# The first 128 tokens' experts start beside the last seven query tiles, in a ring of six buffers

## The chip, the core and the metric

The kernel runs on one core of one Trainium2 chip. The time is that of the device in microseconds, for one execution; 3375.86 us is the median of three (3374.03 to 3380.77). TensorE is called PE in the profile, VectorE DVE, ScalarE ACT, GpSimd POOL, and SP issues most plain loads. A GpSimd queue starts the gathers.

## What is computed

A transformer block with attention, then a second block of gated recurrences, and at its end a layer of product-key experts for 512 tokens of 1024 numbers. Only the last part matters here, cut from the reference:

```python
def _peer(x, w_pq, sub_keys, expert_u, expert_v):
    xf = x.reshape(n_tok, d)
    q = (xf @ w_pq).reshape(n_tok, P_HEADS, 2, P_DHALF)
    s = jnp.einsum('thpd,phkd->thpk', q, sub_keys)
    top_s, top_i = lax.top_k(s, P_TOPK)
    cand_s = (top_s[:, :, 0, :, None] + top_s[:, :, 1, None, :]).reshape(n_tok, P_HEADS, P_TOPK * P_TOPK)
    cand_i = (top_i[:, :, 0, :, None] * N_KEYS + top_i[:, :, 1, None, :]).reshape(...)
    best_s, pos = lax.top_k(cand_s, P_TOPK)
    idx = jnp.take_along_axis(cand_i, pos, axis=-1)
    gate = jax.nn.softmax(best_s)
    ...
    u = expert_u[it]
    h = jax.nn.gelu(jnp.einsum('td,tkd->tk', xt, u), approximate=False)
    v = expert_v[it]
    return jnp.einsum('tk,tkd->td', gt * h, v)
```

and around it `x = x + _peer(_rmsnorm(x, norm2), ...)`, then `_rmsnorm(x, final_norm)`. There are 8 heads, 128 keys in each half, 16 best pairs per head, so 128 experts for each token, out of 16384, each with a row u and a row v of 1024 float32.

## The kernel before

Tokens are taken 128 at a time, one to a partition: four token tiles (`TT`), each with 128 gathers (`PAIRS`). Gather number e brings for each of the 128 tokens the u and v row of its e-th expert, 8 KB per partition. A token tile has four parts (`PARTS`) of 32 gathers, one part for two heads, so there are 16 parts (`NPARTS`).

*Queries.* `project` makes 16 query tiles of 24 matmuls each (line 399 to 401). Weights come in chunks of 512 KB, one to a tile, into a ring of four (`ring`, SP); ScalarE rounds a chunk to its upper half (`upper`, line 956), GpSimd subtracts for the lower (`lower`, line 1962), and that must be there before TensorE's tile. ScalarE's `tile()` waits for a tile to be done and then makes the upper half two chunks further on; then it copies the queries from PSUM to `qpk`. `key_scores(n)` (line 886) makes the scores of part n, from query tiles 0 to 3 for part 0, 4 to 7 for part 1, and so on; the next token tile uses them again in the same order. `first_scores` calls it for parts 0 and 1 behind tiles 4 and 8.

*Top-k on VectorE.* `best_keys(n)` (from line 1859) finds the best keys of a part, `best_pairs(n)` (from line 1878) the best sums, the gates and the expert indices; in it VectorE waits for ScalarE's exponential (`gate_exp`, line 1386), which stands behind query tiles 9 and 13 for parts 0 and 1. Parts 0 and 1 run beside the query tiles.

*Between.* A meeting of PE, ACT and DVE (`meet(…, 19)`). ScalarE before it loads `wide`, an identity with zeros about it, then `final_norm` into `fin_g`, and waits for each. Then `by_tokens` transposes the normalised tokens of all four token tiles (line 907) and `tok_copy` copies them (line 1403) to `h2tok`, which lies in the weight ring.

*Experts.* Eight buffers, `uv[:, 0..7]`, each 2048 float32 per partition. For gather number e: GpSimd waits until the products of gather e - 8 are done (`v_used`) and issues (line 2000). VectorE takes them in pairs: two dot products of u rows with the tokens (line 1938), ScalarE's Gelu of both (line 1412), then two diagonal matrices with gelu times gate (line 1943); TensorE multiplies each with the v rows, two halves of 512 columns (line 930, four instructions of the trace for each gather), and sums in PSUM. The first four gathers may start once part 0 has its indices; the fifth waits for all transposes (`tok_mm`). They stand in GpSimd's program behind `lower_all`, all lower halves. `best_keys(n + 2)` runs after the first half of part n's pairs, `best_pairs(n + 2)` after the second. The residual goes into the same sum, by six matmuls with `wide` of 512 columns at the start of a token tile (line 924) and two at its end (line 935); ScalarE and VectorE then normalise and scale (`scale_out`) while the next token tile runs.

Where buffers lie: `uv[:, 0..3]` in two slots of the arena that are free by then; `uv[:, 4..7]` over the normalised tokens and their lower parts, which query tiles and transposes still read.

## Time and profile before

| | us |
|---|---|
| median of three runs | 3375.86 |
| the profiled execution | 3369.78 |
| its span | 3368.0 |
| PE busy | 2824.0 (84%) |
| DVE busy | 1806.6 (54%) |
| ACT busy | 918.1 (27%) |
| POOL busy | 1068.8 (32%) |
| line 1938, dot products, x512 | 618.9 |
| line 930, products with v, x2048 | 979.5 |
| line 2000, gathers, x512: GpSimd's time | 556.5 |

The query tiles begin near 1905 us of the span and the expert loop near 2020; it lasts to 3353. An engine's busy time says what it did; what it waited for stands in the idle time before an instruction, in brackets with the releaser. GpSimd's time for a gather is that of its issue; the rows land later. Numbers of pairs count from 0: pair p is gathers 2p and 2p + 1, and pair 63 is the last of the first token tile.

### The profile page before, as it was taken

The page shows a single profiled execution, that of the slowest core. Times are in us where ns is not written, and L with a number is a line of the kernel's source. Part 1 is how long each engine was busy: PE and PEld are TensorE (multiplying, and loading weights), DVE is VectorE, ACT ScalarE, POOL GpSimd, SP SyncE. Part 2 cuts the span into 40 slices and gives each one's busy share as a digit, 9 for nine tenths or more (in the row PEclk, how much of TensorE's full clock was granted, in tenths as well). Part 3 has the DMA queues.
Part 4 walks back from the last instruction along what each step waited for, and adds up shares of the span by engine and source line. Part 5 has one row for each costly group of instructions (what it writes and reads, how often), then busy time and mean ns, then how long its engine had stood idle before and what let it go on. Part 6 is the DMA issues. An engine that isn't in the chain of part 4 may idle for free.

```text
span 3368.0 us, 32768 instructions
## 1 busy us (share of the span) xinstructions
PE 2824.0 (84%) x11178; PEld 1867.2 (55%) x11178; DVE 1806.6 (54%) x3673; ACT 918.1 (27%) x1517; POOL 1068.8 (32%) x722
## 2 busy tenths in 40 slices
PE   5988899998998988999789987777777777777776
PEld 3866588785667976779767663333333333333332
DVE  1056233303666633239633237777777777777765
ACT  3244422223655134233543321111111111111100
POOL 2300244441000002345233334444444444444342
PEclk9999999998998999999999989998998899999999
DMA  3200122222110001221112229999999999999998
GB/s 118 78 20 1 51 94 93 87 100 106 69 63 13 1 26 63 88 94 45 63 69 86 90 106 413 396 396 395 408 396 396 401 412 396 398 398 407 401 400 341
DMA packets 115300, 671.68 MB, mean 199 GB/s; under 512 B 16232, under 2 KB 17512, under 8 KB 49008
## 3 DMA queue, kind: packets, MB, share of 16 engines
q0 software_dynamic: 73728, 536.90, 38.9%
q1 hardware_dynamic: 31536, 114.83, 9.6%
q10 hardware_dynamic: 9920, 18.42, 1.6%
q8 instruction: 70, 1.15, 0.1%
q14 instruction: 46, 0.38, 0.0%
HBM read 663.78 MB, written 6.32 MB: 199 GB/s over the span
## 4 chain that ended last, share of the span: by engine, by line
PE 44%; issue 24%; DMA 14%; DVE 13%; ACT 3%; POOL 2%; DVEq 0%; ACTq 0%; PEldq 0%; POOLq 0%; PEld 0%
PE ps L930 14%; DMA arena<-in_experts,arena 13%; PE ps L399 8%; PE ps L400 8%; PE ps L401 8%; POOL ring_r L1962 2%; DVE arena L1938 1%; PE ps L565 1%; DVE arena L1790 1%; PE ps L537 1%; PE ps L456 1%; DVE arena L1943 1%; DVE arena L1789 1%; DVE arena L1772 1%; PE ps L563 1%
## 5 line engine op out<-in xcount | busy, mean ns | idle before, releaser
L930 PE MATMUL ps<-arena 128*128 128x512 f32 x2048 | 979.5, 632 | 319.6 <-DVE arena L1943 319.5
L1962 POOL TENSOR_TENSOR ring_r<-ring,w_hi 128x1024 fp32r<-128x1024 f32 x191 | 470.2, 2462 | 1422.9 <-ACT w_hi L956 1299.0
L930 PEld LDWEIGHTS ps<-arena 128*128 128x128 f32 x2048 | 399.9, 202 | 892.6 <-DVE arena L1943 447.5
L2000 POOL DMA_INDIRECT arena<-in_experts,arena x512 | 556.5, 1087 | 793.5 <-PE ps L930 737.6
L1938 DVE SCALAR_TENSOR_TENSOR arena<-arena,ring 128x1024 f32<-128x1024 f32 x512 | 618.9, 1224 | 265.9 <-DMA arena<-in_experts,arena 237.6
L399 PE MATMUL ps<-n_hi,w_hi 128*128 128x512 f32 (+1 forms) x1264 | 503.5, 398 | 50.6 <-DVE low L1441 20.5
L401 PE MATMUL ps<-n_hi,ring_r 128*128 128x512 f32 (+1 forms) x1264 | 493.6, 391 | 0.0
L956 ACT ACTIVATE w_hi<-ring 128x1024 fp32r<-128x1024 f32 x175 | 185.1, 1058 | 651.2 <-PE ps L401 642.2
L400 PE MATMUL ps<-slot_r,w_hi 128*128 128x512 f32 x896 | 359.1, 401 | 0.0
L1412 ACT ACTIVATE hgel<-hdot 128x2 f32<-128x2 f32 x256 | 52.0, 203 | 1109.2 <-DVE arena L1938 1109.2
L399 PEld LDWEIGHTS ps<-n_hi,w_hi 128*128 128x128 f32 x1264 | 240.6, 190 | 132.1 <-issue 50.8
L401 PEld LDWEIGHTS ps<-n_hi,ring_r 128*128 128x128 f32 x1264 | 240.8, 191 | 54.2
L1943 DVE TENSOR_SCALAR arena<-con,hgel,arena 128x128 f32<-128x128 f32 x512 | 157.5, 389 | 107.9 <-ACT hgel L1412 107.7
L400 PEld LDWEIGHTS ps<-slot_r,w_hi 128*128 128x128 f32 x896 | 173.2, 193 | 39.0 <-issue 1.4
L400 PE MATMUL ps<-low,w_hi 128*128 128x512 f32 (+1 forms) x496 | 188.1, 379 | 0.0
L1461 DVE SCALAR_TENSOR_TENSOR arena<-arena,par 128x512 f32<-128x512 f32 x16 | 11.8, 746 | 185.2 <-ACT arena L996 185.2
L400 PEld LDWEIGHTS ps<-low,w_hi 128*128 128x128 f32 x496 | 93.9, 189 | 17.6
L1552 DVE TENSOR_TENSOR arena<-gtmp,ps 128x512 f32 (+1 forms) x22 | 15.1, 688 | 154.5 <-PE ps L401 154.5
L399 PE MATMUL ps<-slot_r,w_hi 128*128 128x512 f32 x192 | 80.1, 417 | 17.6 <-DVEq L303 17.6
L1127 ACT ACTIVATE w_hi<-ring 128x1024 fp32r<-128x1024 f32 x40 | 42.5, 1062 | 170.2 <-PE ps L401 170.2
L1412 ACT ACT_TABLE_LOAD x60 | 77.0, 1283 | 5.1 <-issue 1.1
L401 PE MATMUL ps<-slot_r,ring_r 128*128 128x512 f32 x192 | 77.0, 401 | 0.0
(322 smaller groups left out, 3758.4 us busy)
## 6 DMA issues: line engine op xcount, KB each, us to landing
ring<-in_weights SPq DMA_DIRECT2D x215, 512.0 KB, 3.5
arena<-in_experts,arena POOLq DMA_INDIRECT x512, 12.5
arena<-low_rest ACTq DMA_DIRECT2D x2, 2048.0 KB, 10.4
h_all<-in_xT ACTq DMA_DIRECT2D x1, 2112.0 KB, 16.4
h_rest<-h_all ACTq DMA_DIRECT2D x1, 2048.0 KB, 7.5
low_rest<-slot_r ACTq DMA_DIRECT2D x1, 2048.0 KB, 7.4
h_all<-h_rest ACTq DMA_DIRECT2D x1, 2048.0 KB, 8.6
out<-w_hi_f SPq DMA_DIRECT2D x4, 512.0 KB, 7.6
```

What stands on the lines that cost most here:

```text
L399: mm(out, x[0], y[0], start=start, stop=False)
L400: mm(out, x[0], y[1], start=False, stop=False)
L401: return mm(out, x[1], y[0], start=False, stop=stop)
L456: last = mm(ps[:, 6 + half, 0:hw], ones, src[:, k, half * hw:half * hw + hw], start=(k == 0), stop=(k == DT - 1))
L930: last = mm(ps[:, yb + half, :], diag[:, j, :], uv[:, j, D + half * 512:D + half * 512 + 512], start=False, stop=False)
L956: fn(w_hi[:, n % PAIR], ring[:, n % RING], ACT.Copy).then_inc(hi_ready, 1)
L1127: fn(w_hi[:, (c0 + j) % PAIR], ring[:, (c0 + j + 2) % RING], ACT.Copy).then_inc(hi_ready, 1)
L1412: fn(hgel[:, 2 * g:2 * g + 2], hdot[:, 2 * g:2 * g + 2], ACT.Gelu).then_inc(s["gelu"], 1)
L1938: last = v.scalar_tensor_tensor(uv[:, sl, 0:D], uv[:, sl, 0:D], 1.0, h2tok[t], ALU.mult, ALU.mult, accum_out=hdot[:, sl:sl + 1])
L1943: v.tensor_scalar(diag[:, sl, :], ident, hgel[:, sl:sl + 1], gates[:, t, bass.ds(i * UV + (first * UV % PAIRS + sl), 1)], ALU.mult, ALU.mu ...
L1962: g_.tensor_tensor(ring_r[:, n % RING], ring[:, n % RING], w_hi[:, n % PAIR].bitcast(F32), ALU.subtract).then_inc(w_ready, 1)
L2000: g_.indirect_dma_start(uv[:, n % UV, :], None, experts, bass.IndirectOffsetOnAxis(ap=idxu[:, n // PAIRS, e:e + 1], axis=0)).then_inc(uv_i ...
```

## The change

It does five things.

- Nine of the 16 query tiles (`EARLY`) run ahead as before. The other seven are put between pairs of the first token tile: `TILE_AT` says before which pair's products TensorE makes which tile. ScalarE's `tile()` and copy stand behind that pair's Gelu. GpSimd's `lower` for the tile after the next stands behind the gathers of the pair two further on. SP's weight loads follow as before, each when its place in the ring is free.
- Part 0's scores come behind tile 3 instead of 4, its exponential behind tile 5 instead of 9. Part 1's scores come behind tile 8, its top-k between pairs (`KEYS_AT`, `PAIRS_AT`: pairs 4 and 8), those of parts 2 to 5 at pairs 18 and 21, 25 and 29, 36 and 40, 52 and 56. The first token tile so has five of each, before four.
- The first token tile uses six buffers (`first_rows`): `uv[:, 0..3]`, a stretch of constants no longer needed, and a new `spare` where `fin_g` was. Its loops are written out, pair by pair. From gather 128 on there are eight again (`rows_of`), in another order, beginning with `uv[:, 4..7]`; the first four need no wait for products. VectorE waits for all products of the first token tile before pair 64.
- Token tile 0 is transposed behind query tile 0, tiles 1 to 3 before pairs 24, 26 and 28.
- `wide` and its load are gone, and so is meeting 19. The residual uses the 128 columns of `ident`, 3 + 1 matmuls for each half; its first six now stand in the first token tile before pair 16, in later ones at the start of the second part. `final_norm` is loaded behind the early tiles, and only `scale_out` waits for it.

The diff, cut to its core:

```diff
+        h2tok = [gtmp[:, :, :].rearrange("p a b -> p (a b)")[:, 0:D]]
+        h2tok += [ring[:, i, :, :].rearrange("p a b -> p (a b)") for i in range(1, TT)]
+        first_rows = [uv[:, 0, :], uv[:, 1, :], uv[:, 2, :], uv[:, 3, :], con[:, level_at:level_at + 2 * D], spare]
+        rows_of = [uv[:, i, :] for i in (4, 5, 6, 7, 2, 3, 0, 1)]
+        UV0 = len(first_rows)
+        EARLY = 9
+        TILE_AT = {1: 9, 4: 10, 7: 11, 11: 12, 14: 13, 17: 14, 20: 15}
+        SCORES_AT = {9: 2, 22: 3, 33: 4, 49: 5}
+        TOKENS_AT = {24: 1, 26: 2, 28: 3}
+        KEYS_AT = {4: 1, 18: 2, 25: 3, 36: 4, 52: 5}
+        PAIRS_AT = {8: 1, 21: 2, 29: 3, 40: 4, 56: 5}
...
-            project(16, (hi2, parts(3)), SEQ, True, first_scores)
-            meet(pe, 19)
-            for t in range(TT):
-                by_tokens(t)
+            for n in range(EARLY):
+                query_tile(n)
+                if n == 0:
+                    by_tokens(0, 0)
+                if n == 3:
+                    pe.wait_ge(keys_in, 16)
+                    pe.wait_ge(evac, TILE["pq"] + 4)
+                    key_scores(0)
+            pe.wait_ge(evac, TILE["pq"] + 8)
+            key_scores(1)
+            pe.wait_ge(s["tok_out"], 2)
+            for pair in range(PAIRS // 2):
+                if pair == PART // 2:
+                    residual(0)
+                if pair in TILE_AT:
+                    query_tile(TILE_AT[pair])
+                if pair in SCORES_AT:
+                    n = SCORES_AT[pair]
+                    pe.wait_ge(evac, TILE["pq"] + min(16, 4 * (n + 1)))
+                    key_scores(n)
+                if pair in TOKENS_AT:
+                    by_tokens(TOKENS_AT[pair], 4)
+                for e in (2 * pair, 2 * pair + 1):
+                    pe.wait_ge(s["diag"], e + 1)
+                    for half in range(2):
+                        last = mm(ps[:, half, :], diag[:, e % UV0, :],
+                                  first_rows[e % UV0][:, D + half * 512:D + half * 512 + 512], start=e == 0, stop=False)
+                    last.then_inc(s["v_used"], 1)
+            residual_end(0)
...
-            act.dma_start(wide, placing).then_inc(consts_in, 16)
-            act.wait_ge(consts_in, 16 * 7)
-            act.dma_start(fin_g, final_norm.partition_broadcast(P)).then_inc(consts_in, 16)
-            act.wait_ge(consts_in, 16 * 8)
-            meet(act, 19)
...
+            act.dma_start(fin_g, final_norm.partition_broadcast(P)).then_inc(consts_in, 16)
+            for pair in range(PAIRS // 2):
+                act.wait_ge(s["dots"], pair + 1)
+                g = pair % (UV0 // 2)
+                fn(hgel[:, 2 * g:2 * g + 2], hdot[:, 2 * g:2 * g + 2], ACT.Gelu).then_inc(s["gelu"], 1)
+                if pair in TILE_AT:
+                    tile()
+                    take_queries(TILE_AT[pair])
+                if pair in TOKENS_AT:
+                    tok_copy(TOKENS_AT[pair], 4)
+                if pair in PAIRS_AT:
+                    gate_exp(PAIRS_AT[pair])
+            finish(0)
...
+            for pair in range(PAIRS // 2):
+                both = (2 * pair, 2 * pair + 1)
+                for e in both:
+                    u_rows = first_rows[e % UV0][:, 0:D]
+                    dve.wait_ge(uv_first[e % UV0], 16 * (e // UV0 + 1))
+                    last = v.scalar_tensor_tensor(u_rows, u_rows, 1.0, h2tok[0], ALU.mult, ALU.mult,
+                                                  accum_out=hdot[:, e % UV0:e % UV0 + 1])
+                last.then_inc(s["dots"], 1)
+                dve.wait_ge(s["gelu"], pair + 1)
...
+                if pair in KEYS_AT:
+                    best_keys(KEYS_AT[pair])
+                if pair in PAIRS_AT:
+                    best_pairs(PAIRS_AT[pair])
+            dve.wait_ge(s["v_used"], PAIRS)
...
-            lower_all(values_at + 8 + PAIR, CHUNKS)
+            lower_all(values_at + 8 + PAIR, queries_at + EARLY)
+            for pair in range(PAIRS // 2):
+                for e in (2 * pair, 2 * pair + 1):
+                    if e >= UV0:
+                        pool.wait_ge(s["v_used"], e - UV0 + 1)
+                    gather(e, first_rows[e % UV0], uv_first[e % UV0])
+                if pair == 2:
+                    lower(queries_at + EARLY, queries_at + EARLY + 1)
+                    lower(queries_at + EARLY + 1, queries_at + EARLY + 2)
+                n = TILE_AT.get(pair - 2, 16) + PAIR
+                if n < 16:
+                    lower(queries_at + n, queries_at + n + 1)
+            pool.wait_ge(s["tok_mm"], TT)
+            pool.wait_ge(chunk_done, CHUNKS)
+            for e in range(PAIRS, TT * PAIRS):
+                n = e - PAIRS
+                if 4 <= n < UV:
+                    pool.wait_ge(s["v_used"], (123, 124, 127, 128)[n - 4])
+                if n >= UV:
+                    pool.wait_ge(s["v_used"], e - UV + 1)
+                gather(e, rows_of[n % UV], uv_in[n % UV])
```

## Rows read from the trace of the kernel before

**Rows 1.** The page: the gather queue (packets, MB, share of 16 engines); weight loads.

```profile
q0 software_dynamic: 73728, 536.90, 38.9%
...
ring<-in_weights SPq DMA_DIRECT2D x215, 512.0 KB, 3.5
```

**Rows 2.** Table of stretches: us, each engine's busy us, clock, DMA share, GB/s.

```profile
2031.00:2095.70 64.70, 50.86 (x110) 20.73 (x108) 45.27 (x114) 7.21 (x17) 30.67 (x29) 0.95 1.01 422
2095.70:2180.60 84.90, 63.08 (x136) 26.64 (x136) 62.80 (x164) 9.75 (x23) 35.59 (x32) 0.90 0.98 396
...
2350.20:3350.00 999.80, 759.73 (x1659) 316.88 (x1660) 739.48 (x1854) 123.75 (x275) 408.57 (x378) 0.92 0.98 403
```

**Rows 3.** Timeline of ScalarE: start us, us, what [idle before <-releaser].

```profile
1911.14 1.06 ACT L956 ACTIVATE w_hi<-ring 128x1024 fp32r<-128x1024 f32 x1 [1.85 <-PE ps L401]
...
1927.88 1.06 ACT L956 ACTIVATE w_hi<-ring 128x1024 fp32r<-128x1024 f32 x1 [4.04 <-PE ps L401]
...
1996.63 0.34 ACTq L1395 DMA_DIRECT2D vnew<-in_placing  x1
2004.36 0.34 ACTq L1397 DMA_DIRECT2D arena<-in_final_norm  x1
```

**Rows 4.** Timeline of TensorE: one set of transposes of four.

```profile
2008.07 1.97 PE L907 MATMUL ps<-con,arena 128*128 128x128 f32 x8 [11.48 <-ACTq L303]
```

**Rows 5.** Timeline of VectorE: first top-k.

```profile
1934.27 0.89 DVE L1859 MAX8 arena<-ps 128x8 f32<-128x128 f32 x4 [24.26 <-PE ps L886]
...
1946.37 3.66 DVE L1904 TENSOR_TENSOR arena<-arena 128x256 f32<-128x256 f32 x4
1964.95 0.19 DVE L1908 TENSOR_REDUCE gsum<-arena 128x2 f32<-128x32 f32 x1 [14.92 <-ACT arena L1386]
...
1966.81 0.18 DVE L1912 CAST arena<-arena 128x32 uint32<-128x32 f32 x1
```

**Rows 6.** Timeline of GpSimd: a splitting, the first gather, the fifth.

```profile
1946.67 2.40 POOL L1962 TENSOR_TENSOR ring_r<-ring,w_hi 128x1024 fp32r<-128x1024 f32 x1 [3.18 <-ACT w_hi L956]
...
1989.23 1.11 POOL L2000 DMA_INDIRECT arena<-in_experts,arena  x1 [0.15 <-issue]
...
2019.80 0.94 POOL L2000 DMA_INDIRECT arena<-in_experts,arena  x1 [25.73 <-PE ps L907]
```

**Rows 7.** Timeline of VectorE: diagonals of pair 2 and of pair 63.

```profile
2030.44 0.76 DVE L1943 TENSOR_SCALAR arena<-con,hgel,arena 128x128 f32<-128x128 f32 x2 [0.39 <-ACT hgel L1412]
...
2349.63 0.62 DVE L1943 TENSOR_SCALAR arena<-con,hgel,arena 128x128 f32<-128x128 f32 x2 [0.39 <-ACT hgel L1412]
```

**Rows 8.** Timeline of GpSimd: gathers about three top-k blocks.

```profile
2099.69 0.93 POOL L2000 DMA_INDIRECT arena<-in_experts,arena  x1 [0.78 <-PE ps L930]
2112.84 1.37 POOL L2000 DMA_INDIRECT arena<-in_experts,arena  x1 [12.21 <-PE ps L930]
...
2143.64 0.94 POOL L2000 DMA_INDIRECT arena<-in_experts,arena  x1 [0.78 <-PE ps L930]
2152.95 1.37 POOL L2000 DMA_INDIRECT arena<-in_experts,arena  x1 [8.38 <-PE ps L930]
...
2365.57 1.03 POOL L2000 DMA_INDIRECT arena<-in_experts,arena  x1 [10.42 <-PE ps L930]
```

**Rows 9.** Table of stretches of 5 us, just behind a `best_pairs`.

```profile
2110.00:2115.00 5.00, 5.00 (x9) 2.05 (x8) 4.23 (x11) 0.41 (x2) 1.37 (x1) 0.65 0.50 193
2115.00:2120.00 5.00, 5.00 (x13) 2.28 (x12) 4.59 (x10) 1.49 (x2) 3.88 (x3) 1.00 0.95 352
```

**Rows 10.** Line 2000, all 512 gathers: issue to landing.

```profile
DMA to landing us min/median/max: 5.3/12.5/15.7
```

**Rows 11.** Timeline of TensorE: a pair's products; residual of tile 1; its end in tile 3.

```profile
2139.66 3.70 PE L930 MATMUL ps<-arena 128*128 128x512 f32 x8 [1.31 <-DVE arena L1943]
...
2356.39 5.32 PE L924 MATMUL ps<-vnew,h_all 128*128 128x512 f32 x12
...
3357.48 1.88 PE L935 MATMUL ps<-vnew,h_all 128*128 128x512 f32 x4
```

More of the change, by code:

```diff
@@ L914, in _ @@
+            residual_end(0)
+            for n in range(PARTS, NPARTS):
                 t = n // PARTS
@@ new lines, in _ @@
+            for n in range(EARLY):
+                if n == 3:
+                    act.wait_ge(chunk_done, count["chunk"] + 1)
+                    take_queries(n)
+                    tile()
+                else:
+                    tile()
+                    take_queries(n)
+                if n == 0:
+                    tok_copy(0, 0)
+                if n == 5:
+                    gate_exp(0)
+            act.dma_start(fin_g, final_norm.partition_broadcast(P)).then_inc(consts_in, 16)
@@ L1408, in _ @@
+            finish(0)
+            for n in range(PARTS, NPARTS):
                 t = n // PARTS
```

141 lines of the change are left out of this document (79 added, 62 removed).

## The prediction, made before the changed kernel was run

> **What bounds the kernel now.** I read the page first, for bytes and queues, then the table of stretches, then the timelines of ScalarE, VectorE, GpSimd and TensorE around the end of the query projection, and last two single blocks inside the expert loop. The expert loop is 512 gathers on one queue [rows 1]. In its first quiet stretch the DMA engines are full at 422 GB/s, and over the long rest they are 98% busy at 403 GB/s, with TensorE at 76% and VectorE at 74% [rows 2]. A gather moves 128 rows of 8 KB, 1.049 MB, so at 422 GB/s it takes 2.485 us and a pair 4.97 us. DMA bounds the loop wherever its queue is fed. It is not fed at two kinds of place.
>
> The first is the way in. ScalarE takes query tiles 0 to 3 from 1911.1 to 1927.9, so one tile is 5.58 us. After the last tile it waits for two loads, 7.7 and 3.6 us, that end at about 2008 [rows 3]; four sets of transposes with their copies follow, up to 2019.5 [rows 4]. GpSimd issues the first gather at 1989.2 behind its last weight splitting, gets four out, and stands 25.7 us until 2019.8 for the transposes [rows 6].
>
> The second is VectorE's top-k work, which sits between pairs. Behind the latter half of it (`best_pairs`) GpSimd's next gather comes 13.15 us after the last one, where some 3.3 is usual (a pair's 4.97 less the 1.7 between its two gathers); behind the first half (`best_keys`) 9.31 us [rows 8]. So the blocks hold the chain up by about 10 and 6 us. With eight buffers most of this is covered: a DMA share of 0.50 in one slice of 5 us and 352 GB/s in the next [rows 9], which with a like slice behind it makes 4.3 us lost. A part of 32 gathers has one block of each kind and lasts 84.9 us [rows 2], against 79.5 at full rate: 5.4 lost, so about 1.1 falls to `best_keys`.
>
> **The change part by part.** The sum runs from the diagonal of one pair to that of another, on VectorE.
>
> Start. Tiles 0 to 3 end as before, plus 1.0 us for one set of transposes (1.97 at half clock [rows 4]); scores of part 0 now come behind tile 3, not tile 4. So VectorE begins top-k at about 1930.7 instead of 1934.3. Its run to the sum of gates is 15.8 us (1934.3 to 1946.37 + 3.66), the wait of 14.9 us for the exponential goes, since that stands behind tile 5 (about 1943), and 2 us more make the indices [rows 5]: ready near 1949. GpSimd must first split chunk 8: it comes behind tile 6, so it runs about 1948.4 to 1950.8 (2.40 each [rows 6]). First gather: 1951. The shortest landing is 5.3 us [rows 10], and a second gather behind an empty queue comes 3.7 us later (estimate from the stretch after 2019.8). Pair 0's diagonal follows about 2 us after its rows: near 1962.2. Before, pair 2 (the first whose rows are gathered in the free-running stretch) has its diagonal at 2030.4 [rows 7]. The two waits for loads and the last three transposes leave the path; `final_norm` loads under the loop and is first needed after it.
>
> Before, from there to pair 63: 2349.6 - 2030.4 = 319.2 us [rows 7].
>
> After, pairs 0 to 63 at full rate: 63 x 4.97 = 313.1 us. On this come the stalls, and here is the weight of the case: the ring is 6 deep and not 8. A gather in the ring of 8 lands 12.5 us after issue at the median and 5.3 at the least [rows 10]; the 7.2 between is the cover for any delay. A ring two shorter holds two gathers less: 7.5 to landing and 2.2 of cover. In other words, every delay that already used up the cover of 8 costs 4.97 us more.
>
> - `best_pairs` at pairs 21, 29, 40, 56: 4.3 + 4.97 = 9.2 each, 36.9.
> - `best_keys` at 25, 36, 52: its restart at 2152.95 [rows 8] just meets the end of the queued rows, so nearly all of a pair's time is added, 1.1 + 4.7 = 5.8 each, 17.4.
> - Pairs 0 to 21 hold seven query tiles. A tile holds TensorE 5.58 us; of that 1.31 is idle anyway (a pair takes 3.70 and then 1.31 idle [rows 11]), so buffers come free 4.3 us late. After five of them GpSimd also waits for ScalarE's upper half and splits 2.4 us before it may issue, another 1.7. Less the cover of 2.2 that is 3.8 x 5 + 2.1 x 2 = 23. Three 512 KB transfers that fall in no gap (two weight chunks, `final_norm`) take 1.24 each, 3.7. `best_pairs` at 8: 9.2. `best_keys` at 4 and 18 stand beside tiles 10 and 14, where TensorE has its own work, so I take one of the two at 5.8. Sum 42; following each pair through this stretch, where some delays cover each other, I get 39 after adding 1.3 us at each of six restarts for the semaphore that VectorE sees later than the landing. I take 38, bounds 20 (tiles and blocks cover each other fully) and 50 (nothing does).
>
> So pairs 0 to 63 take 313.1 + 36.9 + 17.4 + 38 = 405.4, and pair 63's diagonal comes at 2367.6: 18 us later than before. The head start of 68 us is given back with some on top.
>
> Behind pair 63. `best_pairs` for part 5, which now stands right behind it and costs there about 2.6 us, has moved to pair 56: -2.6. The wait for all 128 rows used is 3.7 us on VectorE, behind which the gelu and diagonals of pair 64 stand; four gathers are out ahead without a wait, so ten buffers cover it: 0. The residual was 12 instructions of 512 columns, 5.32 us, that stood in the stall behind `best_pairs` at the start of a token tile [rows 11] and kept TensorE at its upper clock: GpSimd's idle there is 10.42 us instead of 12.21 [rows 8]. It now comes a part later and narrow; for tiles 2 and 3 that costs 1.8 each: +3.6. At the very end four instructions shrink from 512 to 128 columns, 1.88 us [rows 11] to about 0.5: -1.3. Narrow residuals, transposes at 24, 26, 28 and the scores fit TensorE's 1.31 us of idle per pair and the cover: 0; without cover they are at most 1 us each.
>
> Sum: 18 - 2.6 + 3.6 - 1.3 = +17.7. The profiled execution took 3369.8 (span 3368.0), 6.1 below the median of 3375.9, so I put it on the median: **3393.5**.
>
> Two rules beside the rows. The shortest landing in the trace is 5.3 us [rows 10]. The Trainium skill ("DMA: Bandwidth & Descriptors", Anatomy of one DMA) fits a transfer from GpSimd as 2.0 us and its bytes over 436 GB/s, an estimate of 4.4 us for this gather; by it the cover would be 3.1 and not 2.2, and a dozen stalls 0.9 smaller, 3383 in all. The row is of this kernel and decides.
>
> VectorE's four multiplications in the first top-k took 3.66 us while GpSimd split a chunk [rows 5, 6]. The Trainium skill ("SBUF — State Buffer", Who interferes with whom) says that a VectorE instruction with both inputs in SBUF and a GpSimd one that reads SBUF exclude each other for a whole instruction; the trace agrees. It speaks against the change, which puts five splittings between the pairs; only that of chunk 13 would meet the top-k at pair 8, 2.4 us at most, inside the bounds.
>
> **The rivals.** (A) Six buffers do. Delays are absorbed as with eight, or DMA makes up for them. Then the stalls stay 5.4 per part, five parts, plus 9 for the transfers: 313 + 27 + 9 = 349, pair 63 at 2311, and the time is 3337. The place is GpSimd's wait for used buffers; it decides if a gather lands in well under 5.3 us when the queue is short. For it speaks only that two thirds of a landing is queueing; against it that the slice at 0.50 shows the queue running dry even with eight.
>
> (B) The stalls overlap more than I count: top-k runs while TensorE does tiles, and stalls in the loop are 7 and 3 instead of 9.2 and 5.8, the first stretch 26. Then 313 + 37 + 26 = 376, pair 63 at 2338, 3364. This needs landings of about 4.0 us or a quicker first product after a stall. It reaches from 3357 to 3382.
>
> (C) DMA itself is slower with three gathers out. The slice after the stall has share 0.95 but 352 GB/s [rows 9]. Were it 395 instead of 422 all along the first tile, 64 pairs cost 0.34 more each, 22 us: 3415. Against it: after such slices the rate is back while the queue is still short.
>
> (D) The change does not begin as early as it says: if the first exponential or chunk 8 comes a tile later, the start slips 6 us and is not made up: 3399, and if pair 0 waits for tile 8 and the second scores too, up to 3405.
>
> **How the numbers follow.** Forecast as worked (3383 to 3405) 0.48; A 0.10; B 0.24, of which 0.10 is faster; C 0.12; D 0.06. A measurement of this kernel tells about 0.2%, 7 us, from no change, so faster is below 3369 and slower above 3382.6. Faster 0.10 + 0.10 = 0.20; same 0.14; slower 0.48 + 0.12 + 0.06 = 0.66. The range leaves out A and a tip of C: 3357 to 3417.
>
> **What would show it.** Right: first gather near 1951; pair 0's diagonal near 1962; in the first tile's loop GpSimd's median landing near 7.5 us instead of 12.5; slices near `best_pairs` with DMA nearly empty for more than 5 us; 390 to 415 us from pair 0 to 63; parts of the later tiles still 84 to 85 us. Wrong: DMA share at 0.95 or more between pairs 21 and 63 (A); few stalls at tiles (B); share 1.0 at under 400 GB/s (C); a first gather behind 1956 (D). What would upset all of it is a cover that is not the landing less its minimum, since every stall in the sum is scaled by that one difference.

## The result, and the profile after

The changed kernel takes **3394.31 us** (median of 5 runs, 3391.25 to 3399.07) against 3375.86 for the kernel before on the same chip (5 runs, 3373.55 to 3380.77): a ratio of 1.0058, 95% interval 1.0045 to 1.0071. It is slower by 18.5 us; 17.7 was forecast. Its profiled execution took 3393.87, span 3391.9.

The page of the changed kernel: busy time of the engines, then the DMA share (tenths) and GB/s in 40 slices of 84.8 us, then the gather queue.

```profile
PE 2824.0 (83%) x11178; PEld 1871.5 (55%) x11178; DVE 1815.9 (54%) x3673; ACT 905.5 (27%) x1508; POOL 1068.1 (31%) x722
...
DMA  3200122233220002221122288888999999999998
GB/s 114 81 19 1 50 93 94 91 100 106 69 62 7 1 26 75 87 87 44 57 80 83 85 340 308 325 346 360 415 404 392 389 398 397 395 393 391 402 401 347
...
q0 software_dynamic: 73728, 536.90, 39.0%
```

The rate of the gathers rises one slice earlier (340 GB/s in a slice in which the kernel before has 106), and then stays at 308 to 360 GB/s for five slices before it reaches the 389 to 415 of the rest; only the last slice, in which the kernel ends, is lower. The same packets and bytes take nearly the same share as in [rows 1]. So nothing was added for DMA; it is fed worse for 400 us.

Timeline of VectorE of the changed kernel, the diagonals of pairs 0, 21, 25, 29 and 63 (start us, us, what, idle before and its releaser).

```profile
1967.66 0.60 DVE L2022 TENSOR_SCALAR arena<-con,hgel,arena 128x128 f32<-128x128 f32 x2 [0.27 <-ACT hgel L1489]
...
2108.68 0.60 DVE L2022 TENSOR_SCALAR arena<-con,hgel,arena 128x128 f32<-128x128 f32 x2 [3.15 <-ACT hgel L1489]
...
2136.68 0.60 DVE L2022 TENSOR_SCALAR arena<-con,hgel,arena 128x128 f32<-128x128 f32 x2 [0.27 <-ACT hgel L1489]
...
2161.25 0.69 DVE L2022 TENSOR_SCALAR arena<-con,hgel,arena 128x128 f32<-128x128 f32 x2 [0.27 <-ACT hgel L1489]
...
2366.82 0.60 DVE L2022 TENSOR_SCALAR arena<-con,hgel,arena 128x128 f32<-128x128 f32 x2 [0.27 <-ACT hgel L1489]
```

Pair 63 comes at 2366.8, 17.2 us later than in [rows 7]; 18 was forecast. The first stretch, pairs 0 to 21, takes 141.0 us, the second, 21 to 63, 258.1.

Table of stretches of the changed kernel (us; busy us of PE, PEld, DVE, ACT, POOL; clock; DMA share; GB/s): from about pair 32 to pair 63, the later tiles, and three slices about the `best_pairs` at pair 40.

```profile
2180.60:2366.80 186.20, 128.55 (x273) 53.00 (x271) 124.03 (x320) 11.89 (x37) 72.15 (x67) 0.90 0.89 356
2350.00:3370.00 1020.00, 762.08 (x1674) 320.80 (x1675) 737.95 (x1836) 123.33 (x276) 419.22 (x387) 0.91 0.98 400
...
2240.00:2245.00 5.00, 2.93 (x4) 1.39 (x5) 4.46 (x11) 0.41 (x2) 0.00 (x0) 0.50 0.19 79
2245.00:2250.00 5.00, 5.00 (x9) 2.09 (x9) 3.32 (x8) 0.20 (x1) 2.19 (x2) 0.70 0.38 110
2250.00:2255.00 5.00, 5.00 (x13) 2.09 (x11) 1.23 (x2) 0.00 (x0) 3.25 (x3) 1.00 0.99 370
```

Where eight buffers left one slice at a share of 0.50 [rows 9], six leave two, at 0.19 and 0.38. TensorE's clock falls to 0.50, its lower level of 1.2 GHz, in the first of them, after a slice in which TensorE did nothing. That is no difference between the two kernels: it is also 0.50 from 2107 to 2112 us in the kernel before. GpSimd around this block, same kernel, timeline:

```profile
2233.07 0.94 POOL L2100 DMA_INDIRECT arena<-in_experts,arena  x1 [0.78 <-PE ps L971]
2246.12 1.25 POOL L2100 DMA_INDIRECT con<-in_experts,arena  x1 [12.11 <-PE ps L971]
```

It waits 12.1 us for a used buffer, just as with eight ([rows 8]: 12.21). The block is no longer than before. What differs is how much was queued when it began. All landings from 2109 to 2367 us in the changed kernel:

```profile
DMA to landing us min/median/max: 7.2/9.9/16.3
```

### The profile page after: what moved, and what is told of

Its sections match the earlier page's. It is cut to its first block, busy times and chain, and to the rows that moved or that the text cites. A ratio compares the mean times of both kernels' runs of the same rounds, so it can differ in the third digit from the quotient of the medians.

```text
span 3391.9 us, 32226 instructions
## 1 busy us (share of the span) xinstructions
PE 2824.0 (83%) x11178; PEld 1871.5 (55%) x11178; DVE 1815.9 (54%) x3673; ACT 905.5 (27%) x1508; POOL 1068.1 (31%) x722
## 4 chain that ended last, share of the span: by engine, by line
PE 35%; issue 29%; DMA 14%; DVE 14%; POOL 5%; ACT 3%; DVEq 0%; ACTq 0%; PEldq 0%; POOLq 0%; PEld 0%
DMA arena<-in_experts,arena 14%; PE ps L998 9%; PE ps L414 6%; PE ps L415 6%; PE ps L416 6%; POOL ring_r L2065 4%; PE ps L971 3%; PE ps L988 1%; DVE arena L2017 1%; PE ps L580 1%; DVE arena L2041 1%; DVE arena L1875 1%; POOL arena L2100 1%; PE ps L552 1%; DVE arena L1874 1%
## 5 line engine op out<-in xcount | busy, mean ns | idle before, releaser
L998 PE MATMUL ps<-arena 128*128 128x512 f32 x1440 | 695.4, 637 | 232.6 <-DVE arena L2046 232.5
L2100 POOL DMA_INDIRECT arena<-in_experts,arena x491 | 533.2, 1086 | 744.4 <-PE ps L998 517.6
L998 PEld LDWEIGHTS ps<-arena 128*128 128x128 f32 x1440 | 282.6, 203 | 640.6 <-DVE arena L2046 325.2
L2041 DVE SCALAR_TENSOR_TENSOR arena<-arena,ring 128x1024 f32<-128x1024 f32 x384 | 464.5, 1224 | 196.4 <-DMA arena<-in_experts,arena 187.9
L1021 ACT ACTIVATE w_hi<-ring 128x1024 fp32r<-128x1024 f32 x175 | 185.0, 1058 | 658.9 <-PE ps L416 649.8
L971 PE MATMUL ps<-arena 128*128 128x512 f32 x428 | 212.6, 645 | 69.6 <-DVE arena L2022 69.5
L1503 ACT ACTIVATE hgel<-hdot 128x2 f32<-128x2 f32 x192 | 39.0, 203 | 842.6 <-DVE arena L2041 842.6
L971 PEld LDWEIGHTS ps<-arena 128*128 128x128 f32 x428 | 87.3, 209 | 188.6 <-issue 107.5
L2017 DVE SCALAR_TENSOR_TENSOR arena<-arena,gtmp 128x1024 f32<-128x1024 f32 x107 | 132.4, 1251 | 90.4 <-DMA arena<-in_experts,arena 90.2
L2046 DVE TENSOR_SCALAR arena<-con,hgel,arena 128x128 f32<-128x128 f32 x384 | 117.4, 386 | 78.5 <-ACT hgel L1503 78.5
L1546 DVE SCALAR_TENSOR_TENSOR arena<-arena,par 128x512 f32<-128x512 f32 x16 | 11.8, 749 | 185.2 <-ACT arena L1061 185.2
L1637 DVE TENSOR_TENSOR arena<-gtmp,ps 128x512 f32 (+1 forms) x22 | 15.1, 688 | 154.5 <-PE ps L416 154.5
```

The lines of the kernel that those rows point to most:

```text
L971: last = mm(ps[:, half, :], diag[:, e % UV0, :], first_rows[e % UV0][:, D + half * 512:D + half * 512 + 512], start=e == 0, stop=False)
L998: last = mm(ps[:, yb + half, :], diag[:, j, :], rows_of[j][:, D + half * 512:D + half * 512 + 512], start=False, stop=False)
L1021: fn(w_hi[:, n % PAIR], ring[:, n % RING], ACT.Copy).then_inc(hi_ready, 1)
L1503: fn(hgel[:, 2 * g:2 * g + 2], hdot[:, 2 * g:2 * g + 2], ACT.Gelu).then_inc(s["gelu"], 1)
L2017: last = v.scalar_tensor_tensor(u_rows, u_rows, 1.0, h2tok[0], ALU.mult, ALU.mult, accum_out=hdot[:, e % UV0:e % UV0 + 1])
L2041: last = v.scalar_tensor_tensor(u_rows, u_rows, 1.0, h2tok[t], ALU.mult, ALU.mult, accum_out=hdot[:, sl:sl + 1])
```

## The experiments

All times below go by the diagonals of pairs 0, 21, 63 and 255, and this table is read beside the runs. In us:

```
                 pair 0    0 to 21   21 to 63   63 to 255   median
before           2022.3     106.8      220.5      1003.9    3375.9
after            1967.7     141.0      258.1      1011.9    3394.3
unrolled8        1971.2     140.8      257.1      1010.3    3386.6
ring5            1963.2     154.3      287.6      1007.3    3428.7
ring10           1968.8     140.6      222.9       974.3    3322.0
all_early        2000.9     120.5      259.5      1010.5    3410.7
warm             1969.3     138.4      257.7       993.5    3381.4
early_loads      2010.3     107.7      220.3      1006.1    3363.8
split8           1968.7     127.9      218.8       975.1    3304.8
split10          1970.1     126.8      212.8       973.3    3296.6
early_split10    2001.5     108.0      212.5       974.0    3310.9
halves10         1965.1     129.9      212.5       973.4    3299.3
spread10         1965.9     128.8      216.2       973.2    3301.0
```

At the queue's full rate [rows 2] 21 pairs are 104.4 us, 42 pairs 208.7 and 192 pairs 954. The kernel before had medians of 3372.9 to 3373.7 beside the runs of the experiments, 2 to 3 us below the 3375.9 of the table; the ratios given with each run allow for this.

### The number of buffers: a control, five, and ten

To have the depth of the ring as one number, all 256 pairs are written out and a buffer is taken in the order in which it was used. `unrolled8` does what the changed kernel does.

```diff
-        rows_of = [uv[:, i, :] for i in (4, 5, 6, 7, 2, 3, 0, 1)]
+        buffers = first_rows + [uv[:, i, :] for i in (4, 5, 6, 7)]
+        def ring_depth(e):
+            return 6 if e < PAIRS else 8
```

> The changed kernel with all 256 pairs written out instead of loops, buffers handed on in the order in which they come free, six for the first token tile and eight behind it, as before; VectorE's wait for all products before pair 64 is gone, one for the diagonal buffers comes in its place, and every residual stands at pair 16 of its token tile. A control for the runs that follow. Theory of the cover (a stall costs what it exceeds the time that queued gathers last): same ring depths, same time, 3394 within 7. Rival, that written-out code or the wait at pair 64 costs something: then it shows here as over 7 us either way.

Measured: 3386.57 (3383.94 to 3394.33, 8 runs), before 3372.94, ratio 1.0038 [1.0023, 1.0053]. The stretches agree with the changed kernel's within 4 us, but the median is 7.7 us below 3394.3 (6.8 by the two ratios), where I had allowed 7. So the written-out code may be some microseconds faster by itself, and the next two are read against unrolled8 and not against the changed kernel; each differs from it in one line. In `ring5` the first tile has one buffer less.

```diff
-            return 6 if e < PAIRS else 8
+            return 5 if e < PAIRS else 8
```

> As unrolled8, but five buffers instead of six for the first token tile. Theory of the cover: one buffer less is 2.5 us less cover, and five leave none. In pairs 0 to 63 seventeen delays (ten top-k blocks, seven query tiles) each cost up to 2.5 more, so 30 to 42 us more than unrolled8: 3417 to 3429; beyond that the ring's own round (some 12.3 us against five gathers in 12.4) may begin to set the pace between the stalls, up to 3445. Rival, that depth is not what the first tile lacks: 3387 as with six.

Measured: 3428.74 (3427.09 to 3433.7, 4 runs), ratio 1.0170 [1.0151, 1.0188]. The first tile takes 44 us longer for one buffer less, and the whole 42. The total is at the upper end of what the theory gave, the split is not: between pairs 21 and 63 stand seven blocks, and 30.5 us for seven is 4.4 each, not the 2.5 of one gather. With five buffers more is lost than the blocks' stalls alone: the eight pairs 44 to 52, which have no block between them, take 47.8 us in ring5 and 40.3 in unrolled8.

`ring10` goes the other way: from gather 64 on (pair 32, where the last chunk has been used) it has ten.

```diff
-            return 6 if e < PAIRS else 8
+            return 6 if e < 64 else 10
```

> As unrolled8, but from gather 64 on ten buffers, since the four under the tokens are free by then. Theory of the cover: two (first tile from pair 32: four) buffers more add 5 (10) us of cover. In the first tile two of each top-k block stand behind pair 32 and lose about 8 and 4 us each in the trace of the changed kernel, so 24 us go; in the ten parts of later tiles that still have blocks 5.4 us each were lost with eight buffers, of which the queue running dry was 4 at most, so 30 to 45 go. In all 55 to 65 us less, 3330 to 3340. Rival, that the loss is DMA's own (slow with few gathers out, or slow after a burst): no more than 15 us less, over 3379.

Measured: 3322.01 (3318.98 to 3324.35, 4 runs), ratio 0.9853 [0.9828, 0.9878]: faster than both kernels. Tables of stretches, pairs 32 to 63 and the later tiles, first of unrolled8, then of ring10, then pairs 32 to 63 of ring5:

```profile
2184.10:2369.10 185.00, 131.46 (x273) 54.04 (x271) 124.09 (x321) 11.89 (x37) 69.28 (x67) 0.90 0.89 358
2350.00:3200.00 850.00, 638.41 (x1411) 271.33 (x1410) 629.37 (x1603) 71.28 (x206) 356.85 (x323) 0.91 0.98 399
```

```profile
2181.30:2332.30 151.00, 120.70 (x273) 51.95 (x271) 122.29 (x321) 11.89 (x37) 74.53 (x64) 0.92 1.01 421
2350.00:3200.00 850.00, 661.52 (x1467) 283.34 (x1465) 659.16 (x1678) 70.05 (x209) 373.82 (x338) 0.90 1.01 415
```

```profile
2199.30:2405.20 205.90, 142.11 (x264) 56.70 (x264) 124.63 (x321) 11.90 (x37) 72.74 (x64) 0.84 0.85 320
```

The same 31 pairs with the same four blocks take 205.9, 185.0 and 151.0 us with five, six and ten buffers, at 320, 358 and 421 GB/s. Full rate is 154.1; ring10 comes out 3 us below it because 421 GB/s for 151.0 us is 60.6 gathers of the 62, so that more than one had landed before the stretch began. The busy time of VectorE, whose blocks hold up the chain, is the same (124.6, 124.1, 122.3). This is the cause that the forecast rested on, shown by changing it alone. The later tiles gain 36 us more by going from eight to ten, within the 30 to 45 expected; the first tile gains 34.2 between pairs 21 and 63, where I had expected 24.

### Where the seven tiles stand

`all_early` keeps six buffers and everything else of the change, but runs all query tiles ahead of the first pair.

```diff
-        EARLY = 9
-        TILE_AT = {1: 9, 4: 10, 7: 11, 11: 12, 14: 13, 17: 14, 20: 15}
+        EARLY = 16
+        TILE_AT = {}
```

> The changed kernel with all sixteen query tiles ahead of the pairs, none between them; six buffers in the first token tile as before. It measures what the seven tiles cost between pairs against the 39 us that they cost ahead. The first gather should stand behind the splitting of chunk 15, near 1991, and pair 0's diagonal near 2003, 35 us later. If the tiles cost 20 us between pairs, as I reckon, it is 3394 + 35 - 20 = 3409; if they are hidden there, 3429; if they cost as much there as ahead, 3394.

Measured: 3410.69 (3406.62 to 3413.22, 4 runs), ratio 1.0119 [1.0094, 1.0145]. Its first gather (timeline of GpSimd):

```profile
1990.23 1.12 POOL L2101 DMA_INDIRECT arena<-in_experts,arena  x1 [0.17 <-issue]
```

Pair 0 is 33.3 us later than in the changed kernel, and pairs 0 to 21 are 20.5 shorter, close to the 35 and 20 expected. So seven tiles (39 us of TensorE) cost 20.5 between the pairs and 33.3 ahead of them: that part of the change is worth 12.8 us in the trace and 16 in the medians. The delay at pair 63 now splits by the table, with before, all_early and after side by side: no wait for loads and transposes ahead of pair 0, 21.4 earlier; the first tile on six buffers, 380.0 instead of 327.3, 52.7 later; tiles between the pairs, 14.1 earlier (12.8 and 1.4 behind pair 21). 52.7 - 21.4 - 14.1 = 17.2, as measured.

`early_loads` takes from the kernel before only the two waits for loads, and keeps its eight buffers.

```diff
+                if n == 2:
+                    act.dma_start(wide, placing).then_inc(consts_in, 16)
+                if n == 4:
+                    act.wait_ge(consts_in, 16 * 7)
+                    act.dma_start(fin_g, final_norm.partition_broadcast(P)).then_inc(consts_in, 16)
...
-            act.dma_start(wide, placing).then_inc(consts_in, 16)
-            act.wait_ge(consts_in, 16 * 7)
```

> The kernel before with one thing changed: the load of the identity with its zeros and that of final_norm are started beside the query tiles, so that nothing waits for them after the last tile. It takes the plainest part of the head start alone. The trace of before shows 11.4 us of waits there, with the transposes, the fifth gather and the full rate behind them: 11 us less than before, 3362. Rival, that the meeting or the transposes' slow clock takes the place of the wait: under 7 us less.

Measured: 3363.75 (3353.54 to 3368.28, 11 runs), ratio 0.9970 [0.9959, 0.9982]. GpSimd's fifth gather:

```profile
2007.76 0.94 POOL L2003 DMA_INDIRECT arena<-in_experts,arena  x1 [12.27 <-PE ps L907]
```

The idle time of 25.73 us [rows 6] is 12.27, and pair 0 is 12.0 earlier. The waits of [rows 3] were on the path, and the gain of 10 us (11 was expected) needs none of the rest of the change.

### TensorE's clock behind a stall

The prediction put 3.6 us on two tile starts whose wide residual no longer kept the clock up. `warm` gives TensorE six matmuls of 512 columns, whose result is not used, at the start of each of parts 5 to 14.

```diff
+                if PARTS < n < NPARTS - 1:
+                    for half in range(6):
+                        mm(ps[:, 4 + half % 2, :], ident, sk[:, 0:4, :].rearrange("p a b -> p (a b)"), start=True, stop=True)
```

> The changed kernel with six extra matmuls of an identity with 512 columns of the keys, into two free PSUM banks, at the start of parts 5 to 14, where TensorE waits some 9 us for a top-k block; nothing reads them. In the kernel before, the residual did this by chance at the start of a token tile: GpSimd's wait there was 10.4 us and not 12.2. Theory: TensorE comes out of the stall at its upper clock and gives the first buffers back 1.8 us sooner, and what lies beyond the cover is paid in full, so 10 x 1.8 = 18 us less, 3376. Rival, that the clock is off the path: no change, 3394.

Measured: 3381.37 (3374.22 to 3387.96, 10 runs), ratio 1.0028 [1.0017, 1.0038]. TensorE and GpSimd of the changed kernel behind a `best_pairs` (part 5), and then of warm at the same place (timelines):

```profile
2452.78 1.50 PE L936 MATMUL ps<-con,h_all 128*128 128x128 f32 x12
2462.65 17.57 PE L998 MATMUL ps<-arena 128*128 128x512 f32 x36 [8.37 <-DVE arena L2046]
...
2466.70 1.37 POOL L2100 DMA_INDIRECT arena<-in_experts,arena  x1 [13.44 <-PE ps L998]
```

```profile
2451.30 5.32 PE L983 MATMUL ps<-arena,con 128*128 128x512 f32 x12
2460.95 17.43 PE L1001 MATMUL ps<-arena 128*128 128x512 f32 x40 [2.99 <-DVE arena L2049]
...
2463.20 1.03 POOL L2103 DMA_INDIRECT arena<-in_experts,arena  x1 [11.42 <-PE ps L1001]
```

Slices of 5 us about the first product behind the block, two of the changed kernel and two of warm (clock, DMA share and GB/s stand at the end):

```profile
2460.00:2465.00 5.00, 2.35 (x3) 1.17 (x4) 4.60 (x9) 0.20 (x1) 0.00 (x0) 0.50 1.01 423
2465.00:2470.00 5.00, 5.00 (x11) 2.15 (x10) 4.23 (x11) 0.41 (x2) 2.31 (x2) 0.86 0.48 139
```

```profile
2458.00:2463.00 5.00, 2.05 (x5) 1.06 (x6) 4.60 (x9) 0.20 (x1) 0.00 (x0) 1.00 1.01 419
2463.00:2468.00 5.00, 5.00 (x13) 2.12 (x12) 4.23 (x11) 0.41 (x2) 3.43 (x3) 1.00 0.93 334
```

TensorE is idle 8.37 us before its first product in the one and 2.99 in the other, whose fill-in work keeps it busy 5.32 us. The granted clock is 0.50 at the first product in the one and 1.00 (2.4 GHz) in the other, and the slice behind it moves 139 and 334 GB/s. GpSimd's gather, which waits for that product, follows 4.1 us after its start in the one and 2.3 in the other; its idle time falls by 2.0 us, as between the two kinds of stall in [rows 8] (1.8). Ten parts give 18.4 us behind pair 63 in the trace. The medians give 13 and the two ratios 10, against 18 expected; the profiled execution of warm (3374.22) was the fastest of its ten, so the trace overstates the sum. The price per stall at this place and the sign of the sum are shown, its size only to within 10 to 18 us.

### The blocks themselves

If stalls come from long blocks, shorter blocks need fewer buffers. `split8` is unrolled8 with the top-k of a part cut into eight pieces of some 2 us, one every other pair. `split10` has also ring10's ten buffers.

```diff
-            def best_keys(n):
+            def find_best(n):
...
+                yield
...
-                if pair in PAIRS_AT:
-                    best_pairs(PAIRS_AT[pair])
+                if pair in PIECES_AT:
+                    n = PIECES_AT[pair]
+                    work[n] = work.get(n) or find_best(n)
+                    next(work[n], None)
```

> As unrolled8 (six buffers, then eight), but the top-k of a part is cut into eight pieces of about 2 us, one behind every second pair (part 1: every pair), with the scores and the exponential moved to suit. The work is the same. Theory of the cover: a piece of 2 us less the 1.5 us that VectorE idles per pair fits even a cover of 2 us, so the stalls of both kinds go: 21 us in the later parts (first tile), 5 each in ten parts behind it, and 8 to 15 in pairs 0 to 21: 3387 - 45 - 50 - 12 = 3280, between 3270 and 3300. Rival, that VectorE's work and not its blocks fills the time: no more than 20 us less.

Measured: 3304.80 (3303.68 to 3308.51, 4 runs), ratio 0.9799 [0.9782, 0.9817].

> As split8 with ten buffers from gather 64 on. Theory of the cover: with nothing left to cover, two buffers more bring nothing: within 7 us of split8, and DMA full at 422 GB/s from pair 21 on. If split8 keeps stalls, this is the faster by as much as they are.

Measured: 3296.60 (3292.74 to 3300.78, 4 runs), ratio 0.9772 [0.9754, 0.9790], the fastest of all. Tables of stretches, split8 from pair 32 to 63, and split10 for the same pairs and for the later tiles:

```profile
2154.90:2315.50 160.60, 120.78 (x264) 48.63 (x264) 121.47 (x310) 11.89 (x37) 76.45 (x65) 0.97 1.00 403
```

```profile
2155.30:2309.70 154.40, 118.00 (x265) 47.34 (x264) 121.36 (x309) 11.89 (x37) 73.57 (x64) 0.99 1.01 421
2350.00:3200.00 850.00, 648.24 (x1461) 265.18 (x1462) 661.49 (x1686) 73.03 (x212) 391.32 (x334) 0.97 1.01 418
```

With six buffers and short pieces the DMA share is 1.00, so the stalls are gone: 31 pairs take 160.6 us instead of unrolled8's 185.0. TensorE's clock is higher too (0.97 against 0.90), but ring10 reached full rate with a clock of 0.92, so that is not what fills the queue. I had expected 3280 (3270 to 3300), and it fell short by 5 us of the upper end. The rest is little idle time of the queue and mostly its rate, 403 GB/s with six buffers and 421 with ten. That is 6.2 us for 31 pairs, most of the 8.2 between the two kernels, where I had expected at most 7. The lower rate is not steady. Two neighbouring slices of split8:

```profile
2259.90:2264.90 5.00, 3.60 (x9) 1.44 (x8) 3.52 (x9) 0.20 (x1) 1.96 (x2) 1.00 0.96 339
2264.90:2269.90 5.00, 3.18 (x8) 1.17 (x7) 3.68 (x8) 0.20 (x1) 1.47 (x2) 1.00 1.01 426
```

Over these 31 pairs its slices of 5 us run from 339 to 428 GB/s, those of split10 from 411 to 428. Why the rate dips for a few microseconds with six buffers, at a share of 0.96 or more in all slices but the last, is open.

Is the early start still worth something once the stalls are gone? `early_split10` is split10 with all query tiles ahead of the pairs and ten buffers from gather 12.

```diff
-            return 6 if e < 64 else 10
+            return 6 if e < 12 else 10
...
-        EARLY = 9
-        TILE_AT = {1: 9, 4: 10, 7: 11, 11: 12, 14: 13, 17: 14, 20: 15}
+        EARLY = 16
+        TILE_AT = {}
```

> As split10 (top-k in pieces, ten buffers), but all sixteen query tiles ahead of the pairs as in all_early, the transposes of token tiles 1 to 3 at pairs 1 to 3, and ten buffers from gather 12. It asks what the early start of the changed kernel is worth once its stalls are gone. With six buffers the exchange was: start 35 us later, tiles' 20 us saved, 14 us slower in all. In split10 pairs 0 to 21 take 126.8 against 104.4 at full rate; without tiles they should take about 107, and pairs 21 to 63 the same 213. Theory: pair 0 near 2003, pair 63 near 2323, 13 us behind split10: 3310. Rival, that the tiles cost between pairs what they cost ahead: 3297.

Measured: 3310.89 (3310.54 to 3315.3, 4 runs), ratio 0.9816 [0.9796, 0.9836]. It is 14.3 us slower than split10 (13 was expected): pair 0 is 31.4 later, pairs 0 to 21 are 18.8 shorter. By this a tile costs 2.7 between pairs, and 2.9 in the changed kernel (20.5 for seven), nearly the same. early_split10 also has ten buffers from gather 12 on, so part of the 18.8 may be theirs.

What are these 3 us a tile? Two attempts at them. `spread10` puts the tiles further apart, with one or two more pairs between. The pieces of top-k, the scores and the transposes are moved to suit, and the ten buffers come eight gathers later:

```diff
-        TILE_AT = {1: 9, 4: 10, 7: 11, 11: 12, 14: 13, 17: 14, 20: 15}
+        TILE_AT = {1: 9, 5: 10, 9: 11, 13: 12, 17: 13, 22: 14, 27: 15}
```

> As split10, but the seven tiles stand four to five pairs apart (1, 5, 9, 13, 17, 22, 27) and not three to four, transposes at 28, 30 and 32, part 3's top-k from pair 30, ten buffers from gather 72. Three pairs and a tile are 15.9 us of TensorE against 14.9 of DMA, four pairs and a tile 19.3 against 19.9. Theory: between wide-set tiles TensorE no longer sets the pace and the cover of six buffers is whole again at each, so the 20 us of the first stretch shrink by a third: 3290. Rival, that each tile costs its own 3 us wherever it stands: 3297, or a little more for the longer time with six buffers.

Measured: 3301.03 (3299.18 to 3306.7, 4 runs), ratio 0.9789 [0.9768, 0.9809], not 3290. Pairs 0 to 32, which hold all seven tiles in both kernels, take 189.4 us instead of split10's 185.2. So wider spacing does not bring the third of their cost that I expected. That each tile costs its own wherever it stands is not shown: over early_split10 (164.5 for these pairs) that is 3.0 a tile in split10 and 3.6 in spread10, and the pieces of parts 1 to 3 moved as well.

`halves10` splits a chunk in two instructions of half the length, so that VectorE might come in between.

```diff
+                for ks in (slice(0, DT // 2), slice(DT // 2, DT)):
+                    last = g_.tensor_tensor(ring_r[:, n % RING, ks, :], ring[:, n % RING, ks, :], w_hi[:, n % PAIR, ks, :].bitcast(F32),
+                                            ALU.subtract)
```

> As split10, but the seven splittings that GpSimd makes between gathers are each done in two instructions of half the size. In the changed kernel a dot product of VectorE took 4.16 us and not 1.23 beside such a splitting, and pairs of diagonals 2.15 and not 0.60. Theory of the lock (VectorE waits until GpSimd's instruction is over): with halves VectorE waits 1.2 us at most instead of 2.3, so those operations take 2.5 and 1.6 or less; pairs 0 to 21 shorter by 0 to 6 us, the whole within 6 us of 3297. Rival, mere sharing of bandwidth: their length depends on the overlap and not on where an instruction ends, and stays.

Measured: 3299.31 (3292.58 to 3306.0, 4 runs), ratio 0.9781 [0.9755, 0.9807], the same as split10. Timelines of GpSimd and VectorE in halves10:

```profile
1958.82 4.91 POOL L2069 TENSOR_TENSOR ring_r<-ring,w_hi 128x512 fp32r<-128x512 f32 x4
1961.15 3.67 DVE L2008 SCALAR_TENSOR_TENSOR arena<-arena,gtmp 128x1024 f32<-128x1024 f32 x1 [3.16 <-DMA arena<-in_experts,arena]
...
1978.27 1.27 POOL L2069 TENSOR_TENSOR ring_r<-ring,w_hi 128x512 fp32r<-128x512 f32 x1 [5.63 <-ACT w_hi L1013]
1978.81 0.82 DVE L2015 TENSOR_SCALAR arena<-con,hgel,arena 128x128 f32<-128x128 f32 x1 [3.64 <-ACT hgel L1481]
1979.50 1.27 POOL L2069 TENSOR_TENSOR ring_r<-ring,w_hi 128x512 fp32r<-128x512 f32 x1
1979.55 1.30 DVE L2015 TENSOR_SCALAR arena<-con,hgel,arena 128x128 f32<-128x128 f32 x1
```

The dot product takes 3.67 and the two multiplications of a pair of diagonals 2.04 together, where I had expected at most 2.5 and 1.6. The two cases differ. The dot product starts beside the second of four halves that stand back to back (1958.82 to 1963.73) and ends 1.09 us after the last: it gets no turn between them. In the changed kernel it ends 1.09 us after the second of two whole splittings (1966.29), just so. Of the multiplications the first ends at 1979.62, 0.08 us after the first half, and the second at 1980.85, 0.08 after the second half. So there VectorE does come between, but each multiplication then waits for one half, and the sum is hardly less. The same holds for all five such pairs of diagonals in halves10, and in all four of the changed kernel the first multiplication ends 0.08 us after the splitting. The rival, mere sharing of bandwidth, falls with this: where the instruction ends is tied to where GpSimd's ends.

## Why the prediction was right, point by point

**Start.** Forecast 1951 for the first gather and 1962.2 for pair 0's diagonal; measured 1953.7 and 1967.7. ScalarE, GpSimd and VectorE of the changed kernel, timelines:

```profile
1913.69 1.06 ACT L1021 ACTIVATE w_hi<-ring 128x1024 fp32r<-128x1024 f32 x1 [1.85 <-PE ps L416]
```

```profile
1951.14 2.40 POOL L2065 TENSOR_TENSOR ring_r<-ring,w_hi 128x1024 fp32r<-128x1024 f32 x1 [3.17 <-ACT w_hi L1021]
1953.70 1.11 POOL L2100 DMA_INDIRECT arena<-in_experts,arena  x1 [0.17 <-issue]
...
1961.64 4.64 POOL L2065 TENSOR_TENSOR ring_r<-ring,w_hi 128x1024 fp32r<-128x1024 f32 x2
...
1980.31 2.34 POOL L2065 TENSOR_TENSOR ring_r<-ring,w_hi 128x1024 fp32r<-128x1024 f32 x1 [4.77 <-ACT w_hi L1021]
```

```profile
1933.17 0.89 DVE L1944 MAX8 arena<-ps 128x8 f32<-128x128 f32 x4 [20.61 <-PE ps L901]
...
1963.22 4.16 DVE L2017 SCALAR_TENSOR_TENSOR arena<-arena,gtmp 128x1024 f32<-128x1024 f32 x1 [2.40 <-DMA arena<-in_experts,arena]
...
1980.84 2.15 DVE L2022 TENSOR_SCALAR arena<-con,hgel,arena 128x128 f32<-128x128 f32 x2 [3.63 <-ACT hgel L1489]
```

The order was right: the first gather stands right behind a splitting, and VectorE's first top-k runs on to the sum of the gates (1948.95) with no wait for the exponential. Of the 5.5 us by which pair 0 is late, 2.5 come from upstream, since tile 0 ends at 1913.7 where it ended at 1911.1 in the trace of before [rows 3], in code that the change leaves alone. The other 2.9 are a term that I had priced at nothing: two splittings that the change puts behind pair 2's gathers run to 1966.3 while pair 0's rows are read, and a dot product that takes 1.23 alone took 4.16. I had named this exclusion, but counted five splittings between the pairs where the change puts seven, and left out just these two. It reaches the diagonals too: four pairs of them took 2.15 to 2.26 us for their two multiplications instead of 0.60. The rule that I cited (the Trainium skill, "SBUF — State Buffer", Who interferes with whom) is on instructions with both inputs in SBUF; the dot product is one, and the trace agrees with it there. The multiplications of the diagonals have one tensor as input besides two numbers per partition, so that they are held off as well goes beyond what I cited; here the traces alone show it.

**Pairs 0 to 21.** 142.4 was forecast, 141.0 measured, for seven tiles, three transfers, one `best_pairs` and one `best_keys`. all_early shows what of this was the tiles: 20.5 where I had put 23.

**The stalls.** Over full rate the stretches from block to block lost (forecast 9.2 for a `best_pairs`, 5.8 for a `best_keys`):

```
pairs        us     over 4.97 each    block
21 to 25    28.0          8.1         best_pairs
25 to 29    24.6          4.7         best_keys
29 to 36    43.6          8.8         best_pairs
36 to 40    23.8          4.0         best_keys
40 to 52    70.9         11.3         best_pairs, and a second dip 40 us behind it
52 to 56    23.9          4.1         best_keys
56 to 63    43.2          8.4         best_pairs
```

They sum to 49.4, forecast 54.3. That the depth of the ring sets what a block costs is shown by ring5, unrolled8 and ring10; the size is a little off: each `best_keys` cost 1.1 to 1.8 less than I had it. The cover was said to be the landing at the median less the shortest, 7.5 - 5.3 = 2.2. Measured were 9.9 and 7.2, so both are some 2 us higher and their difference is 2.7. The median of the stretch was thus not the 7.5 that I named as a sign, while the difference, on which the sum rests, was near. But the difference is a rough measure of the cover. From pair 21 to 63 it is 5.6 to 8.7 in unrolled8, which does the same work, so 3.1; and with five buffers, where by the sum nothing should be left, it is 5.5 to 7.8, so 2.3. What the runs show is the order of the times with depth, not this formula. By the fit that the Trainium skill gives ("DMA: Bandwidth & Descriptors", Anatomy of one DMA) a gather lands in an estimated 4.4 us, and each stall would be 0.9 smaller, which is near the size of the miss. But its reason, a shorter landing, is not in the trace: none is under 6.8 us between 1953 and 2367, and the shortest of unrolled8 between pairs 21 and 63 is 5.6.

**Rivals.** A (six buffers do) falls with the share of 0.89 and with ring10. B (stalls of 7 and 3, the first stretch 26) falls by its sum, 376 us where 399.1 were measured, and by `best_pairs`, which cost 8.1 to 8.8; but `best_keys` at 4.0 to 4.7 lies about halfway between the 5.8 of the forecast and the 3 of B. C (the queue itself slower with few gathers out) does not hold in the changed kernel: three pairs away from any block take 15.1 us (33 to 36, and 60 to 63), 5.03 each against 4.97 at full rate. Only split8 shows something of it, 403 GB/s at a share of 1.00 where ten buffers have 421. D holds in part: the first gather was 1953.7, 2.7 late, below the 1956 that I had named.

**Behind pair 63** I had -0.3, and the span's end is 6.7 us further from pair 63 than before (1025.1 against 1018.4). Two of three terms hold. The starts of tiles 2 and 3 take 1.3 and 2.9 more, 4.2 for 3.6. That this is the clock is shown only in part: with warm's fill-in work the start of tile 3 takes 4.2 less than in the changed kernel, that of tile 2 only 0.2. The end shrinks by 1.3, to four instructions of 128 columns:

```profile
3382.65 0.61 PE L942 MATMUL ps<-con,h_all 128*128 128x128 f32 x4
```

The gain of 2.6 for the moved `best_pairs` is not seen in full: part 4 went from 82.2 to 81.1. Of the 7.0 that are left, 0.6 and 1.5 are named by this; for about 5 I have no cause. Parts that do the same work differ by more than 2 us between runs (one of them takes 84.0 in all_early, 85.8 in unrolled8 and 86.4 in the changed kernel), so they may be no effect of the change at all. So between the two profiled executions the difference is 24.1 us, 6.4 more than the sum, and between the medians it is 18.5: the profiled execution of before lay 6.1 below its median, that of the changed kernel 0.4. That the forecast met the median within 1 us is in part luck: the start was 5.5 too early, the first stretch 1.4 and the second 4.9 too long, the end 7.0 too short, and the median of the kernel before lies 6.1 above its profiled execution. That the kernel is slower, and by which mechanism, is not luck.

## What to carry to other kernels

A head start before a loop that DMA paces is worth its length only if the loop is then fed as well: here pair 0 came 54.6 us earlier, the first tile on two buffers fewer took back 52.7, and seven query tiles inside it 20.5. How many buffers this ring needs goes by the longest block in the chain that gives them back, here VectorE's top-k, and cutting the block did as much as adding buffers: pieces of 2 us on the same six and eight buffers took the time from 3386.6 to 3304.8, ten buffers alone to 3322.0. A wait for a load ahead of such a loop is the first thing to remove; here it gave 10 us with nothing paid for it.

## What the runs showed of the hardware

- The gather queue at a DMA share of 1.00 moved 403 GB/s with six buffers (339 to 428 in slices of 5 us) and 421 with ten (411 to 428), in split8 and split10.
- Two GpSimd instructions back to back, each splitting a chunk (2.35 us), stretched a VectorE dot product from 1.23 to 4.16 us, and one of them a pair of `TENSOR_SCALAR` from 0.60 to 2.15. The dot product got no turn between instructions back to back, as wholes or as halves (3.67), and ended 1.09 us after the last; each `TENSOR_SCALAR` ended 0.08 us after a whole or a half.
- Six matmuls of 512 columns in a known stall kept the granted clock at 1.00 instead of 0.50 at the first product behind it and shortened GpSimd's wait for a buffer by 2.0 us; ten such stalls gave 18.4 us in the trace and 10 to 13 in the medians.
- Some 40 us behind the `best_pairs` of pair 40 two slices of 5 us (2280 to 2290) fell to 354 and 359 GB/s, after one with a clock of 0.66. The scores of part 5 (1.05 us of TensorE) stand there too; which of the two did it, no run shows.
